# The order of TensorE's three steps in a round of the differential attention

## The reference, cut to what matters

```python
def block(args):                      # q_blk: 128 queries; 12 half-heads of 32, 6 heads of 64
    s = jnp.einsum("bqmd,bkmd->bmqk", q_blk, kf)
    dist = jnp.abs(qpos[:, None] - kpos[None, :])
    p = jax.nn.softmax(s - slopes[:, None, None] * dist, axis=-1)
    p = p.reshape(B, H, 2, Q_BLOCK, S)
    a = p[:, :, 0] - lam * p[:, :, 1]
    return jnp.einsum("bhqk,bkhe->bqhe", a, vf)
```

## Time and profile before

| | us |
|---|---|
| median of 3 runs | 4768.59 (4755.41 to 4770.2) |
| the profiled execution, its own time | 4758.82 |
| its span | 4757.0 |
| PE busy | 4208.0 (88%) |
| DVE busy | 1832.0 (39%) |
| ACT busy | 1226.5 (26%) |
| mean granted TensorE clock, share of full speed | 0.892 |

### The profile page before, as it was taken

One profiled execution on the slowest core, in us unless ns is written; L12 is line 12 of the kernel. 1 busy time (PEld: TensorE's weight loads), 2 busy tenths in 40 slices (PEclk: granted clock), 3 DMA queues, 4 the chain that ended last, 5 costly groups with the idle time before them and its releaser, 6 DMA issues. The chain is left out here.

```text
span 4757.0 us, 58198 instructions
## 1 busy us (share of the span) xinstructions
PE 4208.0 (88%) x22504; PEld 3488.0 (73%) x22504; DVE 1832.0 (39%) x3297; ACT 1226.5 (26%) x2114; POOL 165.1 (3%) x136
## 2 busy tenths in 40 slices
PE   7998888997998888899786787999878879999998
PEld 5777776775777777677475665787655679999997
DVE  2366644233246663523326554332244421111112
ACT  2463223231256222323132112222223311111101
POOL 0240000000032000000000000000000000000000
PEclk9988778998998777899897788999986789999999
DMA  3000001221200000222120001231220024444343
GB/s 121 32 1 1 0 36 71 89 89 51 95 7 1 1 0 36 88 89 88 53 75 1 0 1 73 84 104 67 94 81 0 18 100 169 158 180 159 145 150 124
DMA packets 51456, 324.56 MB, mean 68 GB/s; under 512 B 6528, under 2 KB 7424, under 8 KB 20352
## 3 DMA queue, kind: packets, MB, share of 16 engines
q1 hardware_dynamic: 51328, 322.85, 18.9%
HBM read 319.68 MB, written 2.10 MB: 68 GB/s over the span
## 5 line engine op out<-in xcount | busy, mean ns | idle before, releaser
L490 PE MATMUL bank<-high 128*128 128x512 f32 x2480 | 981.5, 396 | 116.3 <-DVE low L584 81.4
L491 PE MATMUL bank<-low,high 128*128 128x512 f32 x2480 | 977.8, 394 | 0.0
L492 PE MATMUL bank<-high,low 128*128 128x512 f32 x2480 | 976.0, 394 | 0.0
L490 PEld LDWEIGHTS bank<-high 128*128 128x128 f32 x2480 | 473.2, 191 | 224.7 <-issue 67.6
L492 PEld LDWEIGHTS bank<-high,low 128*128 128x128 f32 x2480 | 473.3, 191 | 100.1
L491 PEld LDWEIGHTS bank<-low,high 128*128 128x128 f32 x2480 | 474.0, 191 | 98.6
L548 DVE TENSOR_TENSOR low<-weight_ring,high 128x2048 fp32r<-128x2048 f32 (+1 forms) x144 | 319.3, 2218 | 554.7 <-ACT high L505 554.7
L2851 PE MATMUL bank<-chosen,glu_ring 128*128 128x176 f32 x2816 | 422.2, 313 | 0.0
L2851 PEld LDWEIGHTS bank<-chosen,glu_ring 128*128 128x128 f32 x2816 | 420.0, 190 | 0.1
L505 ACT ACTIVATE high<-weight_ring 128x2048 fp32r<-128x2048 f32 (+1 forms) x144 | 266.5, 1852 | 269.1 <-PE bank L492 230.2
L2862 PE MATMUL bank<-hidden,down_ring 128*128 128x176 f32 x1408 | 211.3, 313 | 0.0
(11 more groups left out here) (464 smaller groups left out, 5169.7 us busy)
## 6 DMA issues: line engine op xcount, KB each, us to landing
glu_ring<-in_w_expert SPq DMA_DIRECT2D x88, 1024.0 KB, 4.9
weight_ring<-in_w_ff SPq DMA_DIRECT2D x64, 1024.0 KB, 4.9
down_ring<-in_w_expert_down SPq DMA_DIRECT2D x64, 704.0 KB, 5.1
weight_ring<-in_w_in SPq DMA_DIRECT2D x22, 1024.0 KB, 4.9
weight_ring<-in_w_ffe SPq DMA_DIRECT2D x22, 1024.0 KB, 4.8
weight_ring<-in_w_downe SPq DMA_DIRECT2D x16, 704.0 KB, 4.1
weight_ring<-in_w_ino SPq DMA_DIRECT2D x11, 1024.0 KB, 4.8
weight_ring<-in_w_ine SPq DMA_DIRECT2D x9, 1024.0 KB, 4.8
```

What stands on the lines that cost most here:

```text
L490: nc.tensor.matmul(mem.bank[b][:, :], whole, high[:, k, :], start=(k == 0), stop=False)
L491: nc.tensor.matmul(mem.bank[b][:, :], whole, low[:, k, :], start=False, stop=False)
L492: last = nc.tensor.matmul(mem.bank[b][:, :], rest, high[:, k, :], start=False, stop=(k == kt - 1))
```

## The change

In PE's list the call `apply(n - 1)` moves from behind `transposed(n)` to the head of the round. Nothing else is edited: every instruction, wait condition, buffer and bank stays, and DVE, ACT, POOL and SP keep their lists.

```diff
             scored(0)
             scored(1)
             for n in range(n_units):
+                if n >= 1:
+                    apply(n - 1)
                 if n + 2 < n_units:
                     scored(n + 2)
                 transposed(n)
-                if n >= 1:
-                    apply(n - 1)
                 if n >= 4 and n % 2 == 0:
                     turn_rows((n - 4) // 2, n)
             apply(n_units - 1)
             for g in range((n_units - 4) // 2, n_units // 2):
                 turn_rows(g, n_units - 1)
```

## The result

| | us |
|---|---|
| the changed kernel, median of 4 runs | 4805.03 (4793.18 to 4813.3) |
| the kernel before, median of 4 runs | 4762.69 (4755.41 to 4770.2) |
| ratio, with its 95% interval | 1.0087 (1.0057 to 1.0117) |
| the profiled execution, its span | 4791.4 (before 4757.0) |

The change costs 0.9%, between 27 and 56 us; 0.6% had been forecast. In the pair of profiles it is 34.4 us, and almost all of that lies in the two attention phases. I measure a phase from its first score product to the end of its last row store: in the kernel before 119.4 us in each layer, in the changed one 136.4 and 136.5. The rest of the program took 4518.1 us in one profile and 4518.5 in the other.

A forecast was written before the change was run, and what follows sets the result against it. PE, busy throughout at full clock, was taken to set the pace. Per layer 2 x 0.34 + 22 x 0.68 - 0.70 = 14.9 us, 29.9 for two, gave a forecast of 4798 us, range 4782 to 4832.

The forecast's parts named there:

- One round at full clock: Value products wait on PE for DVE's first copy of the same unit: a stall of 0.68 us a round.
- The extra matmul beside the stall: First weight load and matmul after each wait: 0 to 0.05 us more a stall, taken as 0, upper end 2.4 us.
- The even rounds: Rounds with row transposes: these wait for the copy, the value products follow with data ready; one stall, not two.
- The end: Round 23: value products of unit 22 cover PE's idle wait for ACT's row store, a gain of 0.70 us a layer.
- The rounds at half clock: Rounds 0 and 1, before the clock rises: a stall of 0.34 us each.
- half a round either way: Clock rise at the phase's start: such a shift costs 1.5 us a layer, 3 in all; 0 taken as likeliest.
- A cold round: A round at half clock in the new order: 8.0 us against 5.1, so 2.9 us for each that stays cold.
- The sum: Stalls of a layer less the gain in the last round: 14.9 us; two layers 29.9.
- The signs: Profile after: `turned` releasing L831's loads, 0.6 to 0.7 us idle each, PE busy some 87%, DVE's idle up 0.7 a round.
- The clock: Attention phase: clock rises late or never, about 4815 to 4926 us, chance 0.11; a fall once up held unlikely.
- Not slower, by the clock behind the phase: Delta net behind the phase: its shift spares up to 10.3 us in three of six sections, giving 4767; chance 0.04.

The follow-up runs named there:

- the wait for both copies: The changed kernel, with the first half of a unit's value products waiting for both of DVE's copies, not the first alone: 4895.4 us, ratio 1.0316.
- S A T: The changed kernel with each round reordered to scores, value products, transposes, and the row transposes behind the next scores: 4809.4 us, ratio 1.0117.

## Why the prediction was right

The time, 4805, lies in the range, and its direction and mechanism were right: a stall behind each T, by the copy of the same unit, with no second wait in the round. By its steps:

*One round at full clock.* From T(2) to T(22), twenty rounds, the kernel before took 212.04 to 297.87, 85.8 us, the changed one 213.06 to 313.63, 100.6: 0.74 us a round where 0.68 was forecast. The difference is the hand-over. I took 0.05 us from ACT to PE for the one from DVE to PE, which takes 0.11: the copy that starts at 213.77 ends at 214.46, and A's first load is at 214.57. That is the mis-sized term, 20 x 0.06 = 1.2 us a layer. Round n = 2 of the changed kernel:

```profile
213.77 1.29 DVE L871 COPY turned<-bank 128x512 f32<-128x512 f32 x2 [2.12 <-PE bank L816]
214.57 1.86 PEld L831 LDWEIGHTS bank<-values,turned 128*128 128x128 f32 x16 [0.71 <-issue]
214.60 1.97 PE L831 MATMUL bank<-values,turned 128*128 128x65 f32 x16 [0.51 <-DVE turned L871]
```

*The extra matmul beside the stall.* Zero, as taken. A's next S comes 1.93 us after A's load (214.57 to 216.50), the same as in an odd round of the kernel before (217.14 to 219.07). The first load after the wait isn't exposed either: its matmul starts 0.03 us behind it, at 214.60.

*The even rounds* have one stall: R waits and A follows 0.12 later. *The end* gave back what was said: A(22) stands where PE had waited for ACT, and from T(22) on the changed phase loses only 0.6 us with two stalls in it. (A stands behind T in the one list and ahead of it in the other; here and in the next item the 1.74 us of that A are left out on both sides, or the loss would be 3.4 us up to T(2) and -1.2 from T(22) on.)

*The rounds at half clock.* Forecast 0.68 us a layer, measured 1.6 up to T(2). The two stalls are there, and the clock rose 2.7 us later than before in the first layer and 3.4 in the second, counted from the phase's start. I had put that shift at "half a round either way" and taken 0: the second mis-sized term, 0.9 us a layer. A cold round, put at 8.0 us, took 8.5 (T at 199.03 and 207.56).

*The sum.* 14.9 us forecast against 16.9 in each layer. The two layers make 34 us, or 0.7%, within the interval of both measurements of this kernel (1.0087 and 1.0081). By the ratios the whole costs 5 to 7 us more than the 34. The phases don't explain that. The runs of either kernel spread by 15 to 23 us along with their mean granted clock, so a few runs can shift a median by as much; which it is stays open.

*The signs.* Of those that I named, PE's idle time before A (0.5, and 0.7 of its loads), its releaser and the full clock came as said. PE was busy for 90% of the full-clock stretch and not 87%, since the recorded ends of the matmuls reach into the gap. DVE's idle time before its copy grew by 1.6 us a round and not by 0.7: I had read the earlier trace rows as one wait of DVE's in a round, where it had two, and the new order makes them one.

*The clock.* I gave a late or falling clock 0.11 and called a fall unlikely, since it had held through a rest of 0.70 at the end of the phase. In the four profiled phases of the changed kernel it didn't fall. But the reasoning was too weak: with the same rests, in the kernel with the changed order from round 12 on, it fell once, and with rests of 1.10 it fell again and again. With the long rests the clock cost 66 to 85 us, as much as the stalls or more. How near the changed kernel is to that is not shown by its own four phases.

*Not slower, by the clock behind the phase.* The two sections of the earlier trace rows took the same in the changed kernel, 28.08 us at 0.87 and 38.50 at 0.51:

```profile
434.52:462.60 28.08, 23.13 (x176) 17.53 (x176) 5.19 (x25) 5.01 (x14) 0.00 (x0) 0.87 0.01 2
1608.60:1647.10 38.50, 33.96 (x177) 24.37 (x177) 5.44 (x26) 5.27 (x14) 0.00 (x0) 0.51 0.00 0
```

So this rival didn't happen: in the pair of profiles the whole rest took the same. That the rest can change is seen elsewhere (4528.5 and 4531.9 us in two of the experiments against 4518.1), and there it got longer.

What was not measured: copies of half the length. In this layout DVE would read a bank while PE writes it. That the stall follows the copy's length is therefore shown from one side only, by the wait for both copies.

## What to carry to other kernels

An order that repeats is judged by which item each step works on, not by which kind of step follows which. Here S, T, A stayed S, T, A, and only the distance between producing and using the copy went from a round to nothing. Put between them at least as much work with old data as the hand-over takes (0.87 us of it removed the stall of 0.74).

A wait on TensorE has a second price. Where the granted clock falls behind it, work that nobody needs can be cheaper than rest, and an experiment that fills the gap with such work separates the two prices.

## What the hardware showed that was not expected

- Six unused products in each gap of 1.3 us made a kernel 66 us faster in its two phases (364.0 to 297.8) and 85 by the ratios (1.0316 to 1.0137), with the granted clock at 1.00, 2.4 GHz, where it had been 0.83 and 0.66 in the two stretches shown.
- A busy TensorE is not enough for the higher clock: in the order S A T it was busy for 125.38 of 129.6 us and stayed at 0.50, 1.2 GHz. In the order of before, where value products follow the transposes at once, it rose 21 us after the first score product; with half of them there, after 31; with full-width identity products behind the transposes, after 17. From the level once reached, S A T held it for 105 us.
- The clock is up before the attention phase (1.00 from 170 to 188 us) and falls at its start; with unused products in the rests there it stayed at 1.00 throughout, and each phase took 5.8 us less.
- The same code with rests of 1.1 us ran at a mean clock of 0.80 over the phase in one layer and 0.63 in the other, 166 against 198 us.
